# Three-pass fp32 projections on one NeuronCore: high and low activations as one 512-column operand, sums of the two halves added outside TensorE

## The chip, the core and the metric

The kernel runs on one core of a Trainium2 chip. The metric is the device time of one launch in microseconds (us); lower is better. The core's engines work on their own instruction streams and meet at semaphores: PE (TensorE, matmuls into PSUM), DVE (VectorE), ACT (ScalarE), POOL (GpSimd) and SP, which starts most DMAs. PSUM has 8 banks of 128 partitions x 512 fp32.

## The reference, cut to what matters

Two transformer blocks over 256 tokens of width 1024, all in fp32. The part that the change touches are the projections whose results are needed with features on the partitions: keys and queries of all attentions, and the input of the pooling mixer.

```python
def memory_attention(xq, mem_k, mem_v): ...     # softmax(q k^T / sqrt(128)) v, 4 heads
def pool_layer(h, w_in, w_group, scale, w_out, mem_k, mem_v):
    proj = h @ w_in
    u, xq = proj[..., :D_MODEL], proj[..., D_MODEL:]
    mix = multiscale_pool(u, w_group, scale)
    return jnp.concatenate([mix, memory_attention(xq, mem_k, mem_v)], axis=-1) @ w_out
def diff_layer(...):    # q, k, v, xq = h @ w_in ; two softmaxes a head, their difference times v
def second_block(...):
    proj = rms_norm(x, g_pre_mix) @ w_in         # q, k, v of MoBA and of retention
    mq, mk = rotary(mq), rotary(mk)              # rq, rk too
    ...
    c = cross_attention(h, mem_n, w_cq, w_ckv, w_co)
```

Between these mixers stand five gated feed-forward layers (1024 x 5632 and 2816 x 1024 each), which the change leaves alone.

## The kernel before, in words

**Arithmetic.** Each fp32 product is made of three matmuls of a rounded type (fp32r): a number is split into a high part and a low part (the rest), and high x high, high x low and low x high are summed in PSUM. ACT makes the high part of a chunk of weights (`w_hi`, L1468), DVE the low part (`w_lo`, L1702).

**Chunks.** All weights come as 238 blocks of 128 x 2048 numbers through a ring of three slots. `Plan` lists them with all other work; every engine walks the same list of items, so the order on each engine is that of the list. A "cols" chunk (`project`) is a projection with features first: 8 contraction tiles (kt) x 2 halves of 128 output features x 3 passes = 48 matmuls, each with 128 x 128 weights standing and 256 tokens moving (`column_passes`, L1119 to L1121). There are 34 such chunks: 10 around the pooling layer (2 keys, 2 queries xq, 4 of u, 2 more keys), 10 in the differential attention (4 q, 4 k, 2 xq), 6 at MoBA and retention (q0, k0, q2, k2, k4, k6 below), 4 keys of the second memory, and 4 queries of the cross-attention. Other chunks have the activations standing and 512 columns of weights moving (`token_passes`, L1125 to L1129, 24 matmuls a chunk).

**Banks.** Two PSUM banks, prod0 and prod1, hold products. A cols chunk fills one of them with both halves (256 + 256 columns); the next takes the other. DVE reads a finished bank in one instruction (L1874, L1876, or two at L1880) that multiplies by `rb`, the token's 1/rms, and signals `prod_read`. So a bank has a whole chunk's time to be read. `rb` is made by PE and ACT at a "spread" item (L1441, L1645) from a statistic that POOL finishes (L1062).

**Order around a cols chunk.** ACT and DVE first split the weights of a later chunk ("flush"), then take the chunk's result. In the attention layers a chunk is "opened": PE does part 0 (kt 0 to 3), then a "tick" of attention work (scores S, weighted values V, transposes T), then part 1. DVE's share of a tick is maxima (L1825, L1821), softmax weights (L1787 to L1802) and low parts of outputs (L1813). Rotation of q and k (L1989 to L1992) and the pooling windows (L2006 to L2017) are DVE work that stands between the chunks. The first chunk that takes new activations is "fresh": PE waits for each low part `acts_l` (L1728).

## Time and profile before

| what | value |
|---|---|
| median of 3 runs | 1423.87 us (1423.79 to 1424.02) |
| span of the profiled execution | 1422.5 us |
| PE busy | 1405.2 us, 99% |
| DVE busy | 856.5 us, 60% |
| ACT busy | 704.0 us, 49% |
| mean granted TensorE clock | 1.000 |

The span runs from the first to the last instruction; the timed runs are 1.4 us longer, which is what lies around it. Busy time of PE counts overlapping matmuls once; a matmul's own duration is longer than its step to the next one, so paces are read from starts. "Idle before" names what an engine waited for.

### The profile page before, as it was taken

The page shows a single profiled execution, that of the slowest core. Times are in us where ns is not written, and L with a number is a line of the kernel's source. Part 1 is how long each engine was busy: PE and PEld are TensorE (multiplying, and loading weights), DVE is VectorE, ACT ScalarE, POOL GpSimd, SP SyncE. Part 2 cuts the span into 40 slices and gives each one's busy share as a digit, 9 for nine tenths or more (in the row PEclk, how much of TensorE's full clock was granted, in tenths as well). Part 3 has the DMA queues.
Part 4 walks back from the last instruction along what each step waited for, and adds up shares of the span by engine and source line. Part 5 has one row for each costly group of instructions (what it writes and reads, how often), then busy time and mean ns, then how long its engine had stood idle before and what let it go on. Part 6 is the DMA issues. An engine that isn't in the chain of part 4 may idle for free.

```text
span 1422.5 us, 18638 instructions
## 1 busy us (share of the span) xinstructions
PE 1405.2 (99%) x7200; PEld 1189.8 (84%) x7200; DVE 856.5 (60%) x1029; ACT 704.0 (49%) x975; POOL 255.9 (18%) x504
## 2 busy tenths in 40 slices
PE   8999999999999999999999999999999999999998
PEld 6888889988888888888889888888887989788886
DVE  5655565756555565555656565555796655565554
ACT  6545455355444454444555555444655554544442
POOL 1022210002222222222012113222200100132222
PEclk9999999999999999999999999999999999999999
DMA  9756554455665656665544347665544554356562
GB/s 355 276 195 218 198 186 174 152 204 174 220 215 197 210 202 209 210 218 200 179 149 150 120 173 267 207 224 206 183 168 146 191 179 136 138 196 231 198 220 74
DMA packets 71223, 275.55 MB, mean 194 GB/s; under 512 B 17344, under 2 KB 37184, under 8 KB 40288
## 3 DMA queue, kind: packets, MB, share of 16 engines
q1 hardware_dynamic: 56736, 259.57, 51.8%
q0 software_dynamic: 14400, 14.81, 3.4%
q8 instruction: 57, 0.93, 0.3%
q14 instruction: 30, 0.25, 0.1%
HBM read 259.88 MB, written 1.05 MB: 183 GB/s over the span
## 4 chain that ended last, share of the span: by engine, by line
PE 93%; ACT 2%; DVE 2%; DMA 1%; issue 1%; SPq 0%; POOL 0%; DVEq 0%; POOLq 0%; ACTq 0%
PE prod L1125 15%; PE prod L1129 15%; PE prod L1126 15%; PE acc L1129 10%; PE acc L1125 10%; PE acc L1126 10%; PE prod L1119 4%; PE prod L1120 4%; PE prod L1121 4%; PE acc L1323 1%; DMA raw<-in_weights_dram 1%; ACT w_hi L1468 1%; PE acc L1144 1%; PE acc L1343 1%; DVE w_lo L1702 1%
## 5 line engine op out<-in xcount | busy, mean ns | idle before, releaser
L1702 DVE TENSOR_TENSOR w_lo<-raw,w_hi 128x2048 fp32r<-128x2048 f32 x235 | 538.1, 2291 | 402.2 <-ACT w_hi L1468 399.8
L1468 ACT CAST w_hi<-raw 128x2048 fp32r<-128x2048 f32 x235 | 447.9, 1907 | 434.1 <-PE prod L1129 179.7
L1125 PE MATMUL prod<-w_hi,acts_h 128*128 128x512 f32 x944 | 370.6, 393 | 3.1 <-DVE four L1858 1.1
L1129 PE MATMUL prod<-w_hi,acts_l 128*128 128x512 f32 x944 | 367.7, 390 | 0.0
L1126 PE MATMUL prod<-w_lo,acts_h 128*128 128x512 f32 x944 | 367.4, 389 | 0.0
L995 POOL DMA_DIRECT2D four<-four x408 | 200.1, 498 | 608.6 <-DVE four L1862 591.5
L1125 PE MATMUL acc<-w_hi,mix_h 128*128 128x512 f32 x600 | 236.1, 394 | 0.0
L1129 PE MATMUL acc<-w_hi,mix_l 128*128 128x512 f32 x600 | 233.7, 390 | 0.0
L1126 PE MATMUL acc<-w_lo,mix_h 128*128 128x512 f32 x600 | 233.5, 389 | 0.0
L1125 PEld LDWEIGHTS prod<-w_hi,acts_h 128*128 128x128 f32 x944 | 177.2, 188 | 44.8 <-issue 6.2
L1129 PEld LDWEIGHTS prod<-w_hi,acts_l 128*128 128x128 f32 x944 | 177.2, 188 | 37.5 <-DVE acts_l L1772 0.3
L1126 PEld LDWEIGHTS prod<-w_lo,acts_h 128*128 128x128 f32 x944 | 177.3, 188 | 35.8
L1129 PEld LDWEIGHTS acc<-w_hi,mix_l 128*128 128x128 f32 x600 | 112.6, 188 | 23.6
L1125 PEld LDWEIGHTS acc<-w_hi,mix_h 128*128 128x128 f32 x600 | 112.7, 188 | 23.0 <-issue 0.2
L1126 PEld LDWEIGHTS acc<-w_lo,mix_h 128*128 128x128 f32 x600 | 112.7, 188 | 22.8
L1119 PE MATMUL prod<-acts_h,w_hi 128*128 128x256 f32 x424 | 124.0, 293 | 1.1 <-ACT work L1532 0.7
L1121 PE MATMUL prod<-acts_h,w_lo 128*128 128x256 f32 x424 | 119.9, 283 | 0.0
L1120 PE MATMUL prod<-acts_l,w_hi 128*128 128x256 f32 x424 | 119.8, 283 | 0.0
L1547 ACT ACTIVATE four<-prod,stats 128x256 f32<-128x256 f32 x108 | 51.1, 474 | 116.6 <-PE prod L1129 107.4
L1119 PEld LDWEIGHTS prod<-acts_h,w_hi 128*128 128x128 f32 x424 | 81.1, 191 | 3.6 <-issue 2.4
L1120 PEld LDWEIGHTS prod<-acts_l,w_hi 128*128 128x128 f32 x424 | 81.2, 191 | 0.4 <-issue 0.2
L1121 PEld LDWEIGHTS prod<-acts_h,w_lo 128*128 128x128 f32 x424 | 81.0, 191 | 0.0
(275 smaller groups left out, 1181.7 us busy)
## 6 DMA issues: line engine op xcount, KB each, us to landing
raw<-in_weights_dram SPq DMA_DIRECT2D x235, 1024.0 KB, 5.0
four<-four SPq DMA_DIRECT2D x408, 16.0 KB, 2.1
four<-four POOLq DMA_DIRECT2D x408, 16.0 KB, 1.9
raw<-in_weights_dram SPq DMA_DIRECT2D x12, 256.0 KB, 6.7
work<-in_mem_dram POOLq DMA_DIRECT2D x2, 1024.0 KB, 13.0
grow<-in_gain_rows_dram POOLq DMA_DIRECT2D x4, 512.0 KB, 3.6
tabs<-in_tabs_dram POOLq DMA_DIRECT2D x1, 1632.0 KB, 10.0
work<-in_x_t_dram SPq DMA_DIRECT2D x4, 256.0 KB, 5.5
```

The source lines that it names most:

```text
L995: engine.dma_start(mid_moved_to[32 * b:32 * b + 32, a * P:(a + 1) * P], mid_blocks[32 * a:32 * a + 32, b * P:(b + 1) * P]).then_inc(done, 16)
L1119: pe.matmul(out, wh, moving_hi, start=first, stop=False, skip_group_check=True)
L1120: pe.matmul(out, wh, moving_lo, start=False, stop=False, skip_group_check=True)
L1121: return pe.matmul(out, wl, moving_hi, start=False, stop=last, skip_group_check=True)
L1125: pe.matmul(out, still_hi, wh, start=first, stop=False, skip_group_check=True)
L1126: pe.matmul(out, still_hi, wl, start=False, stop=False, skip_group_check=True)
L1129: return pe.matmul(out, still_lo, wh, start=False, stop=last, skip_group_check=True)
L1144: mm = pe.transpose(bank[:, i * S + t * P:i * S + (t + 1) * P], x[:, t, kt * P:(kt + 1) * P], ident)
L1323: mm = pe.matmul(bank[:, at:at + width], dests[q][r0:r1, qt + n, t * P:(t + 1) * P], dests[k][r0:r1, kt + n, 0:width], start=(n == 0), sto ...
L1468: act.copy(w_hi[:, c % RING], raw[:, c % RAW]).then_inc(hi_done, 1)
L1547: act.activation(gate_s[:, t], up_bank(it, t)[:, 0:S], ACT.Silu, scale=rstd["x"][:, t:t + 1]).then_inc(silu_done, 1)
L1702: dve.tensor_tensor(w_lo[:, c % RING], raw[:, c % RAW], w_hi[:, c % RING].bitcast(F32), ALU.subtract).then_inc(lo_done, 1)
```

## The change

A cols chunk now works half by half. Half 0 (128 features) goes to prod0 and half 1 to prod1. For each kt one matmul of the high weights takes the high and the low activations side by side, 2 x 256 = 512 columns (both parts now lie in one tensor, `acts` or `mix`, 8 KB or 12 KB apart), and leaves two sums in the bank: columns 0 to 255 for the high, 256 to 511 for the low activations. Then 8 matmuls of the low weights add to the first sum. So 32 matmuls a chunk stand for 48. ACT copies the second sum to the destination (`correction`), DVE adds the first to it and multiplies by `rb` in a second instruction (`feature_half`). A bank is given back, by `halves_read`, after the add. The old whole-bank read is gone. In a fresh chunk the high matmuls of both halves come first (kt 0-1, 2-3, 4-7) and all low weights last. PE now starts a cols chunk when `w_hi` is there and waits for `w_lo` only ahead of the low weights.

```diff
     def project(self, source, col, dest, at, of="x", mid=None, factors=None):
-        self.chunk("cols", (*source, "cols", col), mid, dest=dest, at=at, of=of, e=self.e, factors=factors,
-                   acts=self.acts if of == "x" else self.mem, free=self.bank_free(1))
+        self.chunk("cols", (*source, "cols", col), mid, dest=dest, at=at, of=of, n=self.read, factors=factors,
+                   acts=self.acts if of == "x" else self.mem, free=self.bank_free(2))
         self.used(of)
-        self.to_read(1)
+        self.read += 1
+        for half in range(2):
+            self.bank_reader.append(("halves_read", 2 * self.read - 1 + half))
+        self.e += 2
...
+                def high_passes(half, kts):
+                    if kts[0] == 0:
+                        reader(pe, it["free"][half])
+                    for kt in kts:
+                        if fresh and half == 0:
+                            pe.wait_ge(lo_done_of, it["acts"] if it["of"] == "mem2" else it["acts"] - KT + kt + 1)
+                        at = kt * COLS + half * P
+                        pe.matmul(prod[half], w_hi[:, slot, at:at + P], both[:, :, base + kt], start=kt == 0,
+                                       stop=False, skip_group_check=True)
+                def low_passes(half):
+                    if half == 0:
+                        pe.wait_ge(lo_done, c + 1)
+                    for kt in range(KT):
+                        at = kt * COLS + half * P
+                        mm = pe.matmul(prod[half][:, 0], w_lo[:, slot, at:at + P], hi[:, base + kt], start=False,
+                                       stop=kt == KT - 1, skip_group_check=True)
+                    mm.then_inc(chunk_used if half else features_done, 1)
+                if fresh:
+                    for kts in (range(0, 2), range(2, 4), range(4, 8)):
+                        for half in range(2):
+                            high_passes(half, kts)
+                        turn_pending()
+                    for half in range(2):
+                        low_passes(half)
+                else:
+                    for half in parts:
+                        high_passes(half, range(KT))
+                        low_passes(half)
+                        turn_pending()
...
+            def correction(it, half):
+                if half:
+                    act.wait_ge(chunk_used, it["c"] + 1)
+                else:
+                    act.wait_ge(features_done, it["n"] + 1)
+                act.copy(feature_out(it, half), prod[half][:, 1]).then_inc(correction_out, 1)
...
+            def feature_half(it, half):
+                out, n = feature_out(it, half), 2 * it["n"] + half + 1
+                dve.wait_ge(correction_out, n)
+                dve.tensor_tensor(out, prod[half][:, 0], out, ALU.add).then_inc(halves_read, 1)
+                dve.wait_ge(halves_read, n)
+                if half == 0:
+                    dve.wait_ge(rb_done, it["rb"])
...
+                    ins = dve.tensor_tensor(out, out, r, ALU.mult)
+                if half:
+                    ins.then_inc(prod_read, 1)
```

On ACT and DVE `correction(0)` and `feature_half(0)` stand behind the flush of the "open" item, or, where a chunk isn't opened, behind the flush of the chunk itself with half 1 right after.

DVE at the entrance of MoBA, before (q0 and k0 are the first two cols chunks on the new x, `work` holds q and k; in brackets what an instruction waits for):

```order
L1928 TENSOR_TENSOR x_res<-x_res,grow 128x512 x3
L1702 TENSOR_TENSOR w_lo<-raw,w_hi 128x2048 [waits hi_done,rstd_done]
L1874 TENSOR_TENSOR work<-prod0,rb 128x512 [waits chunk_used,rb_done]
L1702 TENSOR_TENSOR w_lo<-raw,w_hi 128x2048 [waits hi_done]
L1874 TENSOR_TENSOR work<-prod1,rb 128x512 [waits chunk_used,rb_done]
L1952 SCALAR_TENSOR_TENSOR mix_l<-obuf,vecs,mix_h 128x256 [waits mem_hi] x4
```

The same place on DVE after the change:

```order
L1977 TENSOR_TENSOR x_res<-x_res,grow 128x512 x3
L1746 TENSOR_TENSOR w_lo<-raw,w_hi 128x2048 [waits hi_done,rstd_done]
L1825 TENSOR_TENSOR work<-prod0,work 128x256 [waits correction_out]
L1834 TENSOR_TENSOR work<-work,rb 128x256 [waits rb_done,halves_read]
L1825 TENSOR_TENSOR work<-prod1,work 128x256 [waits correction_out]
L1834 TENSOR_TENSOR work<-work,rb 128x256 [waits halves_read]
L1746 TENSOR_TENSOR w_lo<-raw,w_hi 128x2048 [waits hi_done]
L1825 TENSOR_TENSOR work<-prod0,work 128x256 [waits correction_out]
L2001 SCALAR_TENSOR_TENSOR mix<-obuf,vecs,mix 128x256 [waits mem_hi] x4
```

The add that gives back prod0 stands behind the `w_lo` that waits for `rstd_done`, and the add that gives back prod1 behind the multiply that waits for `rb_done` (k0's other three instructions repeat q0's and are left out).

PE at the same place after the change, from q0's last high matmuls to k0's end (before, k0 was 48 matmuls into prod1 with only `mid_done` and `lo_done` to wait for, and the two matmuls of the spread, L1441, in their middle):

```order
L1196 MATMUL prod1<-acts,w_hi 128x512 x4
L1204 MATMUL prod0<-acts,w_lo 128x256 [waits lo_done]
L1204 MATMUL prod0<-acts,w_lo 128x256 x7
L1204 MATMUL prod1<-acts,w_lo 128x256 x8
L1196 MATMUL prod0<-acts,w_hi 128x512 [waits halves_read,hi_done]
L1196 MATMUL prod0<-acts,w_hi 128x512 x7
L1471 MATMUL aux<-tabs,stats 128x128 [waits rb_done,rstd_done]
L1196 MATMUL prod1<-acts,w_hi 128x512 [waits halves_read]
L1196 MATMUL prod1<-acts,w_hi 128x512 x7
L1204 MATMUL prod1<-acts,w_lo 128x256 x8
```

k0's half 0 now waits for q0's prod0, its half 1 for q0's prod1, and the spread, from which `rb` comes, stands between them.

DVE at the end of the pooling projections, before (behind the read of u's last chunk; L2006 to L2017 are one window of the pooling):

```order
L1702 TENSOR_TENSOR w_lo<-raw,w_hi 128x2048 [waits hi_done]
L1874 TENSOR_TENSOR mem_k<-prod0,rb 128x512 [waits chunk_used,rb_done]
L2006 TENSOR_TENSOR work<-work 128x2x256 [waits prod_read,pooled]
L2006 TENSOR_TENSOR work<-work 128x2x256 [waits dve_step]
L2011 SCALAR_TENSOR_TENSOR work<-work 128x512 [waits dve_step]
```

The same place after:

```order
L1746 TENSOR_TENSOR w_lo<-raw,w_hi 128x2048 [waits hi_done]
L1825 TENSOR_TENSOR mem_k<-prod0,mem_k 128x256 [waits correction_out]
L1834 TENSOR_TENSOR mem_k<-mem_k,rb 128x256 [waits rb_done,halves_read]
L1825 TENSOR_TENSOR mem_k<-prod1,mem_k 128x256 [waits correction_out]
L1834 TENSOR_TENSOR mem_k<-mem_k,rb 128x256 [waits halves_read]
L2055 TENSOR_TENSOR work<-work 128x2x256 [waits prod_read,pooled]
```

One instruction has become four, and PE's next chunk needs the first of them.

## Rows read from the trace of the kernel before

**Rows 1.** Page, parts 1 and 2: busy us; tenths of the granted clock.

```profile
PE 1405.2 (99%) x7200; PEld 1189.8 (84%) x7200; DVE 856.5 (60%) x1029; ACT 704.0 (49%) x975; POOL 255.9 (18%) x504
PEclk9999999999999999999999999999999999999999
```

**Rows 2.** Groups by form, PE: the two groups of cols high passes.

```profile
L1119 PE MATMUL prod<-acts_h,w_hi 128*128 128x256 f32 x424 | 124.0, 293 | 1.1 <-ACT work L1532 0.7 <-DVE acts_l L1728 0.4
L1119 PE MATMUL prod<-mix_h,w_hi 128*128 128x256 f32 x128 | 36.3, 284 | 0.0
```

**Rows 3.** Timeline, PE, in an xq chunk: start, duration, engine, line.

```profile
219.15 0.28 PE L1119 MATMUL prod<-acts_h,w_hi 128*128 128x256 f32 x1
...
222.75 0.28 PE L1119 MATMUL prod<-acts_h,w_hi 128*128 128x256 f32 x1
```

**Rows 4.** Timeline, PE, in a chunk with 512 columns moving.

```profile
178.30 0.39 PE L1125 MATMUL acc<-w_hi,mix_h 128*128 128x512 f32 x1
...
187.14 0.39 PE L1125 MATMUL acc<-w_hi,mix_h 128*128 128x512 f32 x1
```

**Rows 5.** Groups, DVE: whole-bank read, and 256 columns of PSUM with SBUF.

```profile
L1874 DVE TENSOR_TENSOR work<-prod,rb 128x512 f32<-128x512 f32 x14 | 9.6, 688 | 14.5 <-PE prod L1121 14.5
L1813 DVE TENSOR_TENSOR mix_l<-o_bank,mix_h 128x256 fp32r<-128x256 f32 x14 | 5.5, 416 | 0.0
```

**Rows 6.** Line L1645, ACT: copy of 256 columns, ns min/median/max.

```profile
L1645 ACT COPY rb<-aux x6: 363/373/374, 100.9 to 1171.2; 128x256 f32<-128x256 f32 x6
```

**Rows 7.** Timeline, DVE, MoBA's entrance.

```profile
1018.83 2.49 DVE L1928 TENSOR_TENSOR x_res<-x_res,grow 128x512 f32<-128x512 f32 x4
1023.53 2.29 DVE L1702 TENSOR_TENSOR w_lo<-raw,w_hi 128x2048 fp32r<-128x2048 f32 x1 [2.21 <-POOL stats L1062]
1025.74 0.68 DVE L1874 TENSOR_TENSOR work<-prod,rb 128x512 f32<-128x512 f32 x1
...
1038.60 2.28 DVE L1702 TENSOR_TENSOR w_lo<-raw,w_hi 128x2048 fp32r<-128x2048 f32 x1
```

**Rows 8.** Timeline, PE, the same place: k0's start, the spread, the first scores.

```profile
1020.77 0.28 PE L1119 MATMUL prod<-acts_h,w_hi 128*128 128x256 f32 x1
...
1023.64 0.62 PE L1441 MATMUL aux<-tabs,stats 128*128 128x128 f32 x4
1024.02 0.36 PE L1119 MATMUL prod<-acts_h,w_hi 128*128 128x256 f32 x1
...
1039.07 0.93 PE L1323 MATMUL acc<-work 64*128 64x128 f32 x8 [1.03 <-DVE work L1992]
```

**Rows 9.** Windows (us, then busy us of PE, PEld, DVE, ACT, POOL; clock): three stretches.

```profile
254.00:276.00 22.00, 22.00 (x169) 21.25 (x168) 21.29 (x36) 9.42 (x11) 0.00 (x0) 1.00 0.36 122
1023.00:1039.00 16.00, 15.04 (x83) 12.80 (x81) 15.27 (x20) 8.31 (x11) 1.10 (x2) 1.00 0.58 204
1039.00:1078.00 39.00, 38.74 (x294) 33.92 (x294) 35.40 (x84) 21.21 (x47) 0.00 (x0) 1.00 0.49 170
```

**Rows 10.** Timeline, DVE, end of the pooling projections: u read, splits behind it.

```profile
253.62 0.69 DVE L1874 TENSOR_TENSOR work<-prod,rb 128x512 f32<-128x512 f32 x1 [3.94 <-PE prod L1121]
...
258.74 2.29 DVE L1702 TENSOR_TENSOR w_lo<-raw,w_hi 128x2048 fp32r<-128x2048 f32 x1
...
270.76 2.28 DVE L1702 TENSOR_TENSOR w_lo<-raw,w_hi 128x2048 fp32r<-128x2048 f32 x1
```

**Rows 11.** Timeline, PE, the same place: tick before u's last chunk, first chunk behind.

```profile
253.35 0.60 PE L1379 MATMUL o_bank<-four,mem_v 128*128 128x256 f32 x2
...
272.79 0.40 PE L1125 MATMUL prod<-w_hi,mix_h 128*128 128x512 f32 x1
```

**Rows 12.** Timeline, differential attention: split behind k0, PE's wait at q1.

```profile
700.34 1.91 ACT L1468 CAST w_hi<-raw 128x2048 fp32r<-128x2048 f32 x1 [3.63 <-PE prod L1121]
...
714.32 0.35 PE L1119 MATMUL prod<-acts_h,w_hi 128*128 128x256 f32 x1 [0.72 <-ACT work L1532]
```

**Rows 13.** Timeline, DVE, the read of the first chunk of keys.

```profile
201.67 0.68 DVE L1874 TENSOR_TENSOR mem_k<-prod,rb 128x512 f32<-128x512 f32 x1
```

More of the change, by code:

```diff
@@ L281, in bank_free @@
         return [self.bank_reader[e - 2] if e >= 2 else None for e in range(self.e, self.e + n)]
-    def to_read(self, n):
-        for _ in range(n):
-            self.read += 1
-            self.bank_reader.append(("prod_read", self.read))
-        self.e += n
     def ffn_down(self, source, p):
@@ L960, in group_bank, with feature_out @@
             return (prod[it["e"] % 2], prod[(it["e"] + 1) % 2], aux[:].rearrange("p (a b) -> p a b", a=2), o_bank)[g]
+        def feature_out(it, half):
+            if it["dest"] == "u":
+                return padded[:, it["at"] + half, PAD:PAD + S]
+            return dests[it["dest"]][:, it["at"] + half]
         def reader(engine, told):
@@ L1132, in operand @@
                 if of == "x":
-                    return acts_lo, acts_h, acts_l, 0
-                return mem_lo, mix_h, mix_l, mem_base[of]
+                    return acts_lo, acts_h, acts_l, acts, 0
+                return mem_lo, mix_h, mix_l, mix, mem_base[of]
             def turn_half(it, h):
@@ L1176, in columns_chunk @@
             def columns_chunk(it, parts):
-                lo_done_of, hi, lo, base = operand(it["of"])
-                slot, bank = it["c"] % RING, prod[it["e"] % 2]
-                if 0 in parts:
-                    reader(pe, it["free"][0])
-                for kt in [kt for part in parts for kt in range(4 * part, 4 * part + 4)]:
-                    if seen[it["of"]] < it["acts"]:
-                        pe.wait_ge(lo_done_of, it["acts"] if it["of"] == "mem2" else it["acts"] - KT + kt + 1)
-                    for half in range(2):
-                        mm = column_passes(bank[:, half], slot, kt * COLS + half * P, hi[:, base + kt],
-                                           lo[:, base + kt], kt == 0 and half == 0, kt == KT - 1)
-                    if kt == 1:
+                lo_done_of, hi, _, both, base = operand(it["of"])
@@ new lines, in columns_chunk @@
+                slot, c = it["c"] % RING, it["c"]
+                fresh = seen[it["of"]] < it["acts"]
+                def high_passes(half, kts):
[7 more added lines that the diff above has]
+                                       stop=False, skip_group_check=True)
@@ L1277, in chunk @@
                     if it["c"] >= RAW:
-                        pe.wait_ge(lo_done, it["c"] + 1)
+                        pe.wait_ge(hi_done if it["kind"] == "cols" else lo_done, it["c"] + 1)
                     for told in it["late_readers"]:
@@ L1508, in _ @@
                     flush()
+                    if kind == "open" and it["chunk"]["kind"] == "cols":
+                        correction(it["chunk"], 0)
                 elif kind in ("up", "cols", "rows_half", "down", "group"):
@@ L1550, in _ @@
                             flush()
+                    elif kind == "cols":
+                        if not it["opened"]:
+                            correction(it, 0)
+                        correction(it, 1)
                     elif kind == "group":
@@ L1837, in _ @@
                     flush()
+                    if it["chunk"]["kind"] == "cols":
+                        feature_half(it["chunk"], 0)
                 elif kind in ("up", "cols", "rows_half", "down", "group"):
```

46 lines of the change are left out of this document (20 added, 26 removed).

## Prediction

> **What bounds the kernel now.** I read the page first, then groups, then the timeline where DVE is densest. PE is busy 1405.2 us of 1422.5 [rows 1], so the kernel is a queue of matmuls with hardly a gap: a matmul saved shortens the time if nothing new makes PE wait, and each new wait of PE is added in full. DVE is at 60% over the span [rows 1], but not evenly: 21.29 of 22 us at the end of the pooling projections, 15.27 of 16 at MoBA's entrance, 35.40 of 39 in the run behind it [rows 9]. There DVE has no room, and there the change gives it work and lets PE wait for it. The account is therefore: one pace, and then the places where a bank comes back late.
>
> **The pace of a cols chunk.** Matmuls with 256 columns start 3.60 us apart over 30 of them: 0.120 us each [rows 3]. With 512 columns it is 8.84 us over 39: 0.227 us each [rows 4]. So a step is about 0.013 us plus the columns, and joining two saves one 0.013. A chunk takes 48 x 0.120 = 5.76 us now and 16 x 0.227 + 16 x 0.120 = 5.55 us after: 0.21 us less. The groups of high passes hold 424 + 128 = 552 matmuls [rows 2], 34 chunks x 16 and 8 of the pooling's group chunk, which stays. 34 x 0.21 = **7.2 us** less. No row has 512 columns in two pieces 8 KB apart. Bounds: 0.227 as in [rows 4], or two separate steps, 0.240, as in [rows 3], which would take 16 x 34 x 0.013 = 7.2 us back. I take 0.227, since that row is a moving operand of the same size and type.
>
> **What a chunk costs ACT and DVE.** ACT: two copies of 0.37 [rows 6]. DVE: instead of one read of 0.69 [rows 5], two adds of 0.42 (PSUM with SBUF, 256 columns [rows 5]) and two multiplies of the same size. Each multiply waits for its add, so little overlaps: 0.8 us a half, 1.6 a chunk, 1.0 us more than now. A bank comes free after: 0.27 from the end of PE's half to the reader (PE's next matmul at 253.35 [rows 11], the read at 253.62 [rows 10]), copy 0.37, add 0.42, in all 1.1 us, if both engines stand ready. PE wants that bank when the other half, 2.8 us, is done. Normally that is covered. It isn't in a fresh chunk, where half 0 ends only 8 x 0.12 = 0.96 us before half 1, nor where the engine is held up ahead of the add.
>
> **MoBA's entrance (2 chunks, q0 and k0).** Now: k0 starts at 1020.77 in the other bank, while DVE waits for POOL's statistic till 1023.53, splits weights for 2.2 us and reads q0 at 1025.74 [rows 7, 8]; nobody minds. After: (a) q0's last `acts_l` is there when DVE goes on to L1928, 1018.9 [rows 7], as before; behind it PE still has 1 + 4 high and 16 low matmuls, 1.1 + 1.9 = 3.0 us, so q0 ends at 1022.0. (b) k0's half 0 needs prod0, whose add stands behind that same wait and split: 1025.75 + 0.42 = 1026.2. PE stands for 4.2 us. (c) Half 0 runs to 1029.0, the spread to 1029.4 (its place in PE's order, 0.38 long, 1023.64 to 1024.02 [rows 8]). Only then does ACT copy `rb` (1030.1), and DVE multiply, add q0's half 1 and free prod1 at 1031.0. PE stands for another 1.6 us. (d) DVE's chain to the rotated keys, which runs now without a gap from 1023.53 to the end of the rotation at 1038.60 [rows 7, 9] and for which the first scores wait at 1039.07 [rows 8], becomes 3.9 us of waiting for `rb`, 2.0 us of extra instructions and small waits longer, less what overlaps: it ends at 1044.4, the scores start at 1044.9. PE is there at about the same time, so nothing more is lost. Net **+5.8 us**, the pace of both chunks and today's 1.03 us of idle PE included.
>
> **The run behind it (4 chunks).** DVE has 3.6 us free in 39 [rows 9], gets 4 us more, and its order puts the add and multiply of half 0 ahead of the softmax weights and the rotation. Walking the queues with the durations now: the transposes behind k2 wait for weights (about 1.7 us), the scores behind k4 for the rotation (1.7 us). From this go the pace of four chunks, 0.8, and gaps of today and work that hides a part. Net **+1.4 us** at the rows_half chunk behind k6.
>
> **The end of the pooling projections (3 chunks).** Call T the end of u's last but one chunk (253.35 now). From there DVE works without a gap: 253.62 to the end of the split at 270.76 + 2.2 = 272.96 [rows 10], 19.3 us, of which three reads 1.8; the new instructions up to the add that frees the bank for the chunk behind are 4.5 us, and the first starts 0.64 after PE: T + 0.64 + 19.3 - 0.2 idle - 1.8 + 4.5 = T + 22.5. PE gets there now at 272.79, T + 19.4 [rows 11], and could at T + 18.8. It is held three times, each time by prod0 behind a split: about 1.4, 1.9 and 0.5 us. Net **+3.1 us**.
>
> **The differential attention (10 chunks).** q0 is fresh like MoBA's q0: 1.2 us of low passes behind the last `acts_l`. Behind k0 the row is: PE's last matmul, ACT's split at 700.34, DVE's split, maxima, exponentials, PE at 714.32 after 0.72 us of idle [rows 12]; the copy of half 1 (0.37) now stands ahead of that split, so q1 starts 1.1 us later than now in sum. Further on ACT's squares for the head norms stand behind a copy that waits for half 0; then POOL, DVE's scaling and PE's turn come later by 1.2 us. Pace gives back most of the rest. Net **+1.5 us**.
>
> **The other 15 chunks.** Keys of the first memory (2): the read at 201.67 stands behind a split [rows 13], k1 needs the bank at 201.3 and gets it at 202.1: +0.9 net. The last 13: -0.21 each, -2.8, and against it three fresh chunks whose successor waits 0.3 us and one turn of x that comes 0.35 late: -1.9 net.
>
> Sum: 5.8 + 1.4 + 3.1 + 1.5 + 0.9 - 1.9 = **+10.8 us**. The span goes from 1422.5 to 1433.3; with the 1.4 us around it, and equally from the median 1423.9, **1434.7 us**. Weights are no new bound: a chunk of 5.55 us asks no more of the DMAs than today's 512-column chunks (24 x 0.227 = 5.44 us).
>
> **Rivals.**
> (A) *The banks are never missed* (not slower). Mechanism: the add gets done within the other half's 2.8 us everywhere, because DVE's waits and splits turn out movable. Then only the pace is left: 1423.9 - 7.2 = **1416.7 us**. It decides at k0 of MoBA: if PE starts k0's half 0 before 1023.5 it holds. Against it: the order shows the add behind `rstd_done`. A sentence of the Trainium skill speaks for it: TensorE: Matmul & The Clock Gate, HAM oscillation, tells of a kernel in which PSUM double buffering "gave no further gain", which would make its loss free. Here DVE's full stretches [rows 9] contradict that. 6%.
> (B) *Only the entrances bite.* In the dense runs DVE's added work falls into gaps I took as filled. Then MoBA's run, the pooling's end and the differential attention keep their pace (-0.8, -0.6, and +1.2 + 0.4 - 2.1 = -0.5 instead of +1.4, +3.1, +1.5): 1434.7 - 7.9 = **1426.8 us**. For: the replay adds small waits in one direction. Against: 21.29 of 22. 13%.
> (C) *The clock falls in the new pause.* Every row has the granted clock at 1.00 [rows 1, 9] and PE's longest wait in the rows is 1.03 us [rows 8]; one of 4.2 us has no row. At the lower of the two levels k0's half 0 takes 2.8 us more and all of DVE's chain behind it moves: **1437.5 us**, or 1440.3 if half 1 runs so too. The Trainium skill (the same page, Why this matters for your kernels) says that gaps of idle PE between bursts bring the clock down to 1.2 GHz; the trace of before doesn't show it. 15%.
> (D) *The joined operand isn't read at the pace of one.* Two pieces cost two steps: **1441.9 us**. 5%.
>
> **How the numbers follow.** The forecast has 61%, with its own spread of about 3 us either way (eight places, each read to some tenths): 1431.5 to 1438. Range: 1426 to 1440.5; it leaves out A, D, the end of C and the outer half of B's spread. About 0.2% (2.8 us) is what a measurement of this kernel tells from no change. Faster by that, below 1421.0: A, 6%. Within, to 1426.7: half of B and a tail of the forecast, 9%. Slower: 85%.
>
> **What would show each step.** Pace: the high matmuls 0.227 us apart and 0.120 for the low ones; the former at 0.24 means D. Entrance: PE idle some 4 us ahead of q0's successor, released by DVE's add, then some 1.6 us; the first MoBA scores 5.8 us later relative to q0's start. Pooling's end: three waits of PE for the add, together near 4 us. PE not busy: 1422.5 - 1405.2 = 17.3 us now, after it 17.3 + 10.8 + 7.2 = 35 us. Granted clock under 1.00 behind the pause means C. I am wrong if PE's new waits sum to less than 7 us, or if they stand at places other than adds that free a bank, weights and rotations.

## The result

| | before | changed |
|---|---|---|
| median | 1423.94 us (1423.79 to 1424.34, 4 runs) | 1442.51 us (1441.90 to 1442.92, 4 runs) |
| span of the profiled execution | 1422.5 us | 1441.1 us |
| PE busy | 1405.2 us | 1407.6 us |
| PE not busy | 17.3 us | 33.5 us |
| DVE busy | 856.5 us | 886.9 us |

The ratio is 1.0129, 95% interval 1.0118 to 1.0141: 18.6 us slower. The forecast was 10.8 us slower, 1434.7 us, and its range ended at 1440.5 us. The sign and the places were right, the size was not: 7.8 us are missing from it.

The page of the changed kernel, parts 1 and 2, against [rows 1]:

```profile
PE 1407.6 (98%) x6656; PEld 1163.2 (81%) x6656; DVE 886.9 (62%) x1127; ACT 725.7 (50%) x1043; POOL 257.1 (18%) x504
PEclk9999999999999999999999999999999999999999
```

544 matmuls are gone and PE is busy 2.4 us longer; the other 16.2 us are time in which PE isn't busy. The row of the clock shows nothing: a slice is 36 us, and the fall lasted 6.8 us.

PE's waits, with what ended them: us in all, times, longest. These are the first nine rows.

```profile
PE prod L1196 <- DVE work L1825: 6.1, 3, 4.0
PE prod L1196 <- DVE mem_k L1825: 2.5, 2, 1.8
PE acc L1373 <- DVE sq L1850: 1.8, 1, 1.8
PE acc L1163 <- DVE x_res L1809: 1.7, 1, 1.7
PE acc L1353 <- DVE work L2041: 1.4, 1, 1.4
PE prod L1196 <- DVE acts L1772: 1.4, 2, 0.7
PE aux L1373 <- DVE mix L2094: 1.3, 1, 1.3
PE acc L1151 <- DVE x_res L1794: 1.3, 3, 0.5
PE aux L1437 <- POOL mem_v L1042: 1.3, 1, 1.3
```

L1825 is the add that gives a bank back: 8.6 us in its two rows. L1850 are softmax weights, L2041 the rotation: the added work made them late. Not all rows are new: the list of the kernel before has, under its own line numbers, the waits for L1809 (1.7 us), L2094 (1.3) and L1042 (1.3) too. Read this view for the places, not for the sum: small delays don't stand in it, and neither does time at a lower clock.

**MoBA's entrance**, PE (the answer to [rows 8]): q0's high matmuls, k0's half 0, the spread, k0's half 1, the first scores.

```profile
1025.03 2.60 PE L1196 MATMUL prod<-acts,w_hi 128*128 128x512 f32 x8 [0.69 <-DVE acts L1772]
...
1033.55 3.75 PE L1196 MATMUL prod<-acts,w_hi 128*128 128x512 f32 x8 [4.01 <-DVE work L1825]
...
1038.81 0.75 PE L1471 MATMUL aux<-tabs,stats 128*128 128x128 f32 x4
...
1040.88 2.11 PE L1196 MATMUL prod<-acts,w_hi 128*128 128x512 f32 x8 [1.32 <-DVE work L1825]
...
1055.09 0.93 PE L1353 MATMUL acc<-work 64*128 64x128 f32 x8
```

The same eight matmuls take 3.75 us behind the pause of 4.01 us and 2.11 us behind that of 1.32. The windows of this stretch (us, then busy us of PE, PEld, DVE, ACT, POOL; then the granted clock) say why:

```profile
1024.00:1028.00 4.00, 3.31 (x15) 2.14 (x14) 3.98 (x9) 2.40 (x8) 1.89 (x4) 1.00 0.60 203
1028.00:1034.00 6.00, 1.99 (x14) 1.82 (x14) 3.18 (x3) 3.74 (x9) 1.69 (x4) 0.86 0.37 127
1034.00:1037.00 3.00, 3.00 (x8) 2.33 (x8) 0.00 (x0) 0.00 (x0) 0.00 (x0) 0.50 0.94 317
1037.00:1040.00 3.00, 2.56 (x13) 2.27 (x12) 0.00 (x0) 0.74 (x2) 0.00 (x0) 0.65 0.08 33
1040.00:1044.00 4.00, 3.09 (x17) 2.58 (x17) 3.87 (x6) 0.02 (x1) 0.00 (x0) 1.00 0.00 0
```

0.50 is 1.2 of 2.4 GHz. From 1034 to 1037 DVE, ACT and POOL do nothing: they wait for PE, which runs at half its clock. DVE there (the answer to [rows 7]):

```profile
1030.77 2.29 DVE L1746 TENSOR_TENSOR w_lo<-raw,w_hi 128x2048 fp32r<-128x2048 f32 x1 [2.22 <-POOL stats L1069]
1032.98 0.42 DVE L1825 TENSOR_TENSOR work<-prod,work 128x256 f32<-128x256 f32 x1
1040.07 0.42 DVE L1834 TENSOR_TENSOR work<-work,rb 128x256 f32<-128x256 f32 x1 [6.67 <-ACT rb L1689]
1040.41 0.42 DVE L1825 TENSOR_TENSOR work<-prod,work 128x256 f32<-128x256 f32 x1
```

The add of half 0 stands behind the statistic and a split, the add of half 1 behind `rb`, which comes from PE's own spread.

**Where the time went.** Starts of the same instruction of PE in both traces, subtracted; each row is what the shift grew by in that stretch.

| stretch | last pair of starts | measured | forecast |
|---|---|---|---|
| up to the first memory's keys | - | -0.1 | 0 |
| keys of the first memory | 206.73, 207.79 | +1.2 | +0.9 |
| end of the pooling projections | 272.79, 276.43 | +3.0 | +3.1 |
| differential attention | 793.20, 800.46 | +3.6 | +1.5 |
| MoBA's entrance | 1039.07, 1055.09 | +8.8 | +5.8 |
| run behind it | 1070.17, 1088.77 | +2.6 | +1.4 |
| the last 13 chunks | 1203.20, 1221.68 | -0.5 | -1.9 |
| sum | | +18.5 | +10.8 |

The rows are rounded; unrounded they sum to 18.48. The 13 chunks lie in two places: -0.4 at the first xq and u, -0.1 at the second memory and the cross-attention.

**The pace.** Timeline, PE, keys of the second memory in the changed kernel, one row for eight matmuls:

```profile
1148.09 2.08 PE L1196 MATMUL prod<-mix,w_hi 128*128 128x512 f32 x8
1150.01 1.12 PE L1204 MATMUL prod<-mix,w_lo 128*128 128x256 f32 x8
1150.96 2.00 PE L1196 MATMUL prod<-mix,w_hi 128*128 128x512 f32 x8
1152.80 1.12 PE L1204 MATMUL prod<-mix,w_lo 128*128 128x256 f32 x8
```

From start to start a steady half is 1.84 + 0.96 = 2.80 us, 0.230 us a high and 0.120 us a low matmul. A steady chunk takes 5.59 us against 5.76: 0.17 us gained, not 0.21. The fresh chunk ahead of these rows began at 1142.34 and took 5.75 us: nothing gained. Its half 0 is done only 8 low matmuls before PE wants that bank again for the next chunk, so PE is held there.

### The profile page after: what moved, and what is told of

It reads as the page before. It is cut to its first block, busy times and chain, and to the rows that moved or that the text cites. A ratio compares the mean times of both kernels' runs of the same rounds, so it can differ in the third digit from the quotient of the medians.

```text
span 1441.1 us, 17716 instructions
## 1 busy us (share of the span) xinstructions
PE 1407.6 (98%) x6656; PEld 1163.2 (81%) x6656; DVE 886.9 (62%) x1127; ACT 725.7 (50%) x1043; POOL 257.1 (18%) x504
## 3 DMA queue, kind: packets, MB, share of 16 engines
HBM read 259.88 MB, written 1.05 MB: 181 GB/s over the span
## 4 chain that ended last, share of the span: by engine, by line
PE 87%; DVE 6%; ACT 3%; issue 2%; DMA 1%; SPq 0%; POOL 0%; DVEq 0%; POOLq 0%; ACTq 0%
PE prod L1132 15%; PE prod L1136 15%; PE prod L1133 15%; PE acc L1136 9%; PE acc L1132 9%; PE acc L1133 9%; PE prod L1196 6%; PE prod L1204 3%; DVE w_lo L1746 2%; DMA raw<-in_weights_dram 1%; ACT w_hi L1498 1%; PE acc L1353 1%; ACT four L1703 1%; DVE acts L1772 1%; PE acc L1151 1%
## 5 line engine op out<-in xcount | busy, mean ns | idle before, releaser
L1132 PE MATMUL prod<-w_hi,acts 128*128 128x512 f32 x944 | 370.6, 393 | 3.2 <-DVE w_lo L1754 1.2
L1136 PE MATMUL prod<-w_hi,acts 128*128 128x512 f32 x944 | 367.7, 390 | 0.0
L1133 PE MATMUL prod<-w_lo,acts 128*128 128x512 f32 x944 | 367.5, 389 | 0.0
L1132 PE MATMUL acc<-w_hi,mix 128*128 128x512 f32 x600 | 236.1, 393 | 0.0
L1136 PE MATMUL acc<-w_hi,mix 128*128 128x512 f32 x600 | 233.8, 390 | 0.0
L1133 PE MATMUL acc<-w_lo,mix 128*128 128x512 f32 x600 | 233.5, 389 | 0.0
L1132 PEld LDWEIGHTS prod<-w_hi,acts 128*128 128x128 f32 x944 | 177.2, 188 | 44.7 <-issue 7.6
L1136 PEld LDWEIGHTS prod<-w_hi,acts 128*128 128x128 f32 x944 | 177.2, 188 | 37.6 <-DVE acts L1816 0.3
L1133 PEld LDWEIGHTS prod<-w_lo,acts 128*128 128x128 f32 x944 | 177.3, 188 | 35.7
L1136 PEld LDWEIGHTS acc<-w_hi,mix 128*128 128x128 f32 x600 | 112.6, 188 | 23.7
L1132 PEld LDWEIGHTS acc<-w_hi,mix 128*128 128x128 f32 x600 | 112.7, 188 | 22.8
L1133 PEld LDWEIGHTS acc<-w_lo,mix 128*128 128x128 f32 x600 | 112.7, 188 | 22.7
L1196 PE MATMUL prod<-acts,w_hi 128*128 128x512 f32 x416 | 111.9, 410 | 7.8 <-DVE work L1825 5.3
L1196 PEld LDWEIGHTS prod<-acts,w_hi 128*128 128x128 f32 x416 | 75.6, 191 | 27.1 <-issue 7.5
```

What stands on the lines that cost most here:

```text
L1132: pe.matmul(out, still_hi, wh, start=first, stop=False, skip_group_check=True)
L1133: pe.matmul(out, still_hi, wl, start=False, stop=False, skip_group_check=True)
L1136: return pe.matmul(out, still_lo, wh, start=False, stop=last, skip_group_check=True)
L1196: pe.matmul(prod[half], w_hi[:, slot, at:at + P], both[:, :, base + kt], start=kt == 0, stop=False, skip_group_check=True)
```

## Experiments

Lines in the profiles of most variants are up to some tens higher than in the changed kernel; the operations are the same. "Old form" is that of the kernel before. "Shift" is, as in the table, how much later an instruction of PE starts than in the kernel before. Medians are to be held against 1442.51 (changed) and 1423.9 to 1424.3 (before, run each time beside them).

### The entrance

**e1.** q0 and k0 in the old form.

```diff
     def project(self, source, col, dest, at, of="x", mid=None, factors=None):
+        old = self.projects in OLD
...
+        if old:
+            self.bank_reader.append(("prod_read", self.read))
+            self.e += 1
+            return
...
+OLD = [20, 21]
```

> Changed kernel with q0 and k0 at MoBA's entrance in the old form (48 matmuls, one bank, one read by DVE), the other 32 cols chunks in the new form. Theory 1 (the entrance loses through the bank behind DVE's wait and through the clock): the first MoBA scores come 8.8 us earlier than in the changed kernel (their shift against the kernel before is then +7.2, not +16.0), the granted clock stays at 1.00, the time is 1442.5 - 8.8 = 1433.7 us. Rival (DVE's stretch behind the entrance is full in either form, so that PE only waits a little later): less than 6 us come back, 1436.5 us or more, and PE's waits in the four chunks of the run grow by the rest.

Measured: 1433.32 us (1432.9 to 1433.6), 9.2 us less, and the granted clock stays at 1.00 there, both as expected (1433.7). In the trace the shift is 6.9 us when q0 begins and 6.8 us at the first scores. The whole loss of the entrance is local to two chunks of 34.

**e2.** PE's pause filled with matmuls that nobody reads.

```diff
                 elif kind == "open":
+                    if it["fill"]:
+                        reader(pe, it["fill"])
+                        pe.wait_ge(hi_done, it["chunk"]["c"] + 1)
+                        for n in range(30):
+                            pe.matmul(aux[:, 0:S], w_hi[:, it["chunk"]["c"] % RING, 0:P], acts_h[:, n % KT], start=True, stop=True)
                     chunk(it["chunk"], (0,))
```

> Changed kernel with 30 more matmuls of 256 columns into the unused auxiliary bank (30 x 0.12 = 3.6 us of work whose result nobody reads) where PE stood still for 4.0 us ahead of k0's half 0. Theory 1 (the pause is what lowered the clock): granted clock 1.00 there, k0's half 0 takes 2.8 instead of about 5.2 us, the time is 2.5 us less than that of the changed kernel, 1440.0 us. Rival (the fall has another cause, for instance DVE's and ACT's load there, or costs nothing because the chain on DVE decides anyway): 1442.5 us.

Measured: 1440.32 us (1440.15 to 1442.28; three of the four runs lie within 0.2 us, the fourth has no trace). PE's timeline and the window behind:

```profile
1029.32 3.76 PE L1447 MATMUL aux<-acts,w_hi 128*128 128x256 f32 x30
1033.49 2.08 PE L1196 MATMUL prod<-acts,w_hi 128*128 128x512 f32 x8 [0.41 <-DVE work L1830]
...
1038.29 2.11 PE L1196 MATMUL prod<-acts,w_hi 128*128 128x512 f32 x8 [1.33 <-DVE work L1830]
```

```profile
1034.00:1037.00 3.00, 2.97 (x19) 2.49 (x17) 0.00 (x0) 0.37 (x1) 0.00 (x0) 1.00 0.97 328
```

k0's half 0 starts when it did before (1033.49 for 1033.55), runs at full clock, and half 1 starts 2.59 us earlier. The bank came back at the same moment, so nothing but the clock was taken away: it costs 2.6 us at this place (2.2 us between the medians), and a busy PE prevents it. This was rival (C) of the prediction. The Trainium skill (TensorE: Matmul & The Clock Gate, Why this matters for your kernels) says that gaps of idle PE bring the clock down to 1.2 GHz; by that, the traces agree here. The falls behind shorter pauses, in e5 and e8 below, are known from these traces alone.

**e5 and e6.** DVE's wait for the statistic left out; then also one multiply for both halves, behind both adds.

```diff
                         dve.tensor_tensor(x[:, t, cols], x[:, t, cols], grow[:, cols], ALU.mult).then_inc(xf_done, 1)
-                    dve.wait_ge(rstd_done, it["n"] + 1)
...
                 dve.tensor_tensor(out, prod[(it["e"] + half) % 2][:, 0], out, ALU.add).then_inc(halves_read, 1)
+                if not half:
+                    return
                 dve.wait_ge(halves_read, n)
...
+                dve.wait_ge(rb_done, it["rb"])
...
-                if half == 0:
-                    dve.wait_ge(rb_done, it["rb"])
...
+                    ins = dve.tensor_tensor(out, out, bcast(r, 2), ALU.mult)
```

> Changed kernel, DVE doesn't wait for POOL's statistic behind the four multiplies of x at MoBA's entrance (the multiply by rb, which needs that statistic, waits for rb anyway). Its next split of weights can then start at 1028.6 instead of 1030.8 in the changed kernel's own time, and the add behind it 2.2 us earlier. Theory 1 (that wait, passed on by the add, makes PE's pause, and the pause lowers the clock): PE's 4.0 us ahead of k0's half 0 become 1.8, the granted clock stays at 1.00 there, 2.2 + 2.5 us less: 1437.9 us. Rival (ACT's squares and its copies behind them hold the add just as long): the pause stays over 3 us, the clock falls, 1441 us or more.

> As e5_no_stat_wait, and in all 34 chunks DVE adds half 0, later half 1, and multiplies both halves by rb in one instruction of 512 columns behind the second add, so that no add stands behind rb, and 34 instructions go. Theory 1: PE's second wait at the entrance (1.3 us, for the add behind the multiply that needs rb) goes too, and DVE saves about 0.85 - 0.7 = 0.15 us a chunk where it has no room: 1.0 to 1.5 us less than e5_no_stat_wait, 1436.6 us. Rival (the chain to the rotated keys on DVE sets the time there, and the later multiply takes back what the earlier add gives): the same as e5_no_stat_wait.

Measured: e5 1438.47 us (1437.97 to 1440.06), e6 1435.10 us (1434.66 to 1435.50). PE at k0's half 0 and half 1 in e5, and at k0's half 0 in e6:

```profile
1031.60 2.06 PE L1222 MATMUL prod<-acts,w_hi 128*128 128x512 f32 x8 [1.71 <-DVE work L1876]
...
1036.38 2.11 PE L1222 MATMUL prod<-acts,w_hi 128*128 128x512 f32 x8 [1.32 <-DVE work L1876]
```

```profile
1030.07 2.06 PE L1222 MATMUL prod<-acts,w_hi 128*128 128x512 f32 x8 [1.71 <-DVE work L1876]
```

One wait of DVE less takes 2.3 us from the pause, and behind the 1.71 us that are left the clock stays at 1.00: both as expected for e5. But the profiled execution, the longest of the four (1440.06 us; the others 1437.97 to 1438.72), has a fall of the clock elsewhere, in the run, behind a pause of the size that the changed kernel has there too (1.77 us) without a fall. The eight matmuls behind it and the window:

```profile
1067.27 0.63 PE L1399 MATMUL acc<-tabs,sq 128*128 128x128 f32 x3 [1.75 <-DVE sq L1901]
1067.57 3.67 PE L1222 MATMUL prod<-acts,w_hi 128*128 128x512 f32 x8
```

```profile
1068.00:1070.00 2.00, 2.00 (x6) 1.52 (x6) 1.97 (x3) 0.70 (x2) 0.00 (x0) 0.50 0.04 8
```

That costs 1.6 us in this execution, so a pause of some 1.7 us is one that the clock sometimes survives and sometimes doesn't. The kernel before has one too, 1.68 us at 1231.5, with the clock at 1.00.

e6 gained 3.4 us on e5 and not 1.0 to 1.5. Held trace against trace, k0's half 1 starts 1.6 us earlier, of which a new wait behind it takes 1.0 back; the differential attention gives 1.3 us, the run 1.0 us beside the 1.6 of the clock. That was the first sign that the dense stretches had been sized too small. I took it for 0.15 us a chunk less on DVE, come through nearly whole; but the edit also moves 0.43 us of DVE's work from ahead of a tick to behind it, and e14 below speaks for that as the reason.

**e11.** The same wait left out of the kernel before.

> Kernel before, old form in all 34 chunks, with DVE's wait for the statistic behind the four multiplies of x left out, as in e5. Theory 6 (in the kernel before DVE's row from 1023.53 to the rotated keys has no gap, so 2.2 us less of waiting ahead of it moves the first scores until PE's own work bounds them; PE's idle time there is 1.03 us): 1.0 us less, 1423.0 us. Rival (rb, not the wait, starts that row): no change, 1424.0 us.

Measured: 1424.25 against 1424.15 us, ratio 1.0001 (0.9992 to 1.0010). The 1.0 us didn't come; the rival holds. DVE's timeline:

```profile
1020.94 2.28 DVE L1702 TENSOR_TENSOR w_lo<-raw,w_hi 128x2048 fp32r<-128x2048 f32 x1
1025.53 0.69 DVE L1874 TENSOR_TENSOR work<-prod,rb 128x512 f32<-128x512 f32 x1 [2.31 <-ACT rb L1645]
```

The split runs 2.6 us earlier than in [rows 7], and then DVE waits 2.31 us for `rb`. The read of q0 starts at 1025.53 for 1025.74. In the kernel before that wait hid behind another one; it cost time only when a bank's release was put behind it.

### The dense stretches

**e9.** The ten chunks of the differential attention and the four of the run in the old form (as e1, with other numbers in the list).

> Changed kernel with the ten chunks of the differential attention and the four of MoBA's and retention's run (q2, k2, k4, k6) in the old form; the 20 others, MoBA's entrance among them, in the new one. Theory 5 (each place costs by itself what the shift between the two traces shows there): the shift grows by 3.6 us in the differential attention and by 2.6 us in the run, so 6.2 us come back: 1442.5 - 6.2 = 1436.3 us. Rival (in the dense places the loss is the lateness of the entrance and goes with it, or a place that is mended sends its wait on to the next one): less than 4 us come back, 1438.5 us or more.

Measured: 1435.64 us (1435.33 to 1435.90), 6.9 us less (6.2 expected). Against the changed kernel's trace the shift grows by 3.6 us over the differential attention and 2.6 us over the run, the figures of the table. The pause at the entrance is 4.01 us as before and the clock falls as before: the places are independent and add up.

**e14.** The multiply of half 0 left out in those 14 chunks.

```diff
                 if half == 0:
                     dve.wait_ge(rb_done, it["rb"])
+                    if 10 <= it["site"] < 20 or 22 <= it["site"] < 26:
+                        return
```

> Changed kernel without the multiply by rb of half 0 (0.43 us of DVE) in the ten chunks of the differential attention and the four of MoBA's and retention's run; half of the keys and queries is unscaled there, nothing else changes. Theory 5a (in the dense places the loss is DVE's added instruction time, which passes to PE nearly whole: e6 took 0.15 us a chunk from DVE there and the shift grew by 1.3 us less over ten chunks): 14 x 0.43 = 6.0 us less of DVE's time, of which 60 to 90% come back: 1437.1 to 1438.9 us. Rival 5b (the loss there is the place of the add and the copy in the order, and of the splits, not their length): at most 1.5 us come back, 1441 us or more.

Measured: 1439.66 us (1439.20 to 1440.30), 2.9 us less: 47% of the 6.0 us, between the two theories. By place: 1.6 of the 3.6 us in the differential attention, 1.05 of the 2.6 us in the run. PE's waits there, changed kernel, then e14 (end of the differential attention, then softmax weights in the run):

```profile
791.14 0.65 PE L1487 MATMUL aux<-tabs,sq 128*128 128x128 f32 x4 [1.09 <-DVE sq L2079]
...
1071.73 0.55 PE L1373 MATMUL acc<-tabs,sq 128*128 128x128 f32 x3 [1.77 <-DVE sq L1850]
1079.59 0.93 PE L1353 MATMUL acc<-work 64*128 64x128 f32 x8 [1.39 <-DVE work L2041]
```

```profile
1069.14 0.55 PE L1399 MATMUL acc<-tabs,sq 128*128 128x128 f32 x3 [1.18 <-DVE sq L1903]
```

The wait for the weights falls by 0.59 us. So the multiply of half 0, 0.43 of the 1.0 us that the change adds to DVE in a chunk, is a little under half of the loss. Is it its length or its place? e6 keeps a multiply of both halves in these chunks, but behind the tick, and saves 1.3 us in the differential attention and 1.1 us in the run, against 1.6 and 1.05 us with the multiply left out. So most of what it costs is its place ahead of the tick's softmax weights. 1.2 us are the fresh pair q0 and k0 of the differential attention, which e14 leaves unmoved. How the rest divides between the order of copies and adds and the time still added stays open.

### The order of adds and splits

**e7 and e8.** Copy and add of half 0 ahead of the split of weights, in all chunks; e8 with the repairs of e6 as well.

```diff
                 if kind == "open":
-                    flush()
                     if it["chunk"]["kind"] == "cols":
                         feature_half(it["chunk"], 0)
+                    flush()
...
+                    if kind == "cols" and not it["opened"] and not it["old"]:
+                        feature_half(it, 0)
                     if not early:
```

> Changed kernel with its stat wait, but ACT copies and DVE adds and multiplies half 0 of every cols chunk ahead of the split of weights that stood before them. It reaches the chunks without a tick in the middle that have a split there: keys, xq, the end of the pooling projections, the entrances. Theory 4 (at the end of the pooling projections and at the keys of the first memory PE waits since the add stands behind a 2.2 us split): the waits for mem_k's add (2.5 and 0.4 us) go, 2 us of it as time; at MoBA's entrance the add comes 2.2 us earlier, the pause is 1.8 us and the clock stays: 1442.5 - 2.0 - 4.7 = 1435.8 us. Rival (the weights, split later, come late instead): the waits for w_lo grow by as much, 1440 us or more.

> Changed kernel with the three repairs of order together: no wait for the statistic ahead of the adds, one multiply behind both adds, adds ahead of the split. Theory 1 and 4: the entrance costs 1.6 us instead of 8.8, the end of the pooling projections and the keys 2 us less: 1442.5 - 7.2 - 2.5 = 1432.8 us, still slower than the kernel before (1423.9), since DVE has more to do and PE's other waits stay. Rival (order was all that was wrong, the banks are never missed once the adds stand first): 1423 us or less.

Measured: e7 1466.49 us (1464.05 to 1468.26), e8 1453.82 us (1453.51 to 1455.91). The times expected for them were too low by 31 and 21 us. DVE in e7, in u's chunks with a tick:

```profile
244.25 0.42 DVE L1876 TENSOR_TENSOR work<-prod,work 128x256 f32<-128x256 f32 x1 [1.35 <-ACT work L1548]
244.71 0.43 DVE L1885 TENSOR_TENSOR work<-work,rb 128x256 f32<-128x256 f32 x1
245.05 2.28 DVE L1774 TENSOR_TENSOR w_lo<-raw,w_hi 128x2048 fp32r<-128x2048 f32 x1
247.25 0.16 DVE L1899 RECIPROCAL small<-small 128x2 f32<-128x2 f32 x1
247.44 0.62 DVE L1901 TENSOR_SCALAR four<-four,small 128x256 f32<-128x256 f32 x2
```

I had overlooked that a split stands in opened chunks too. DVE now waits for half 0 first, and the split then runs between the add and the softmax weights, for which PE waits. The split needs nothing from the running chunk, so ahead of the add it fills that wait. By place, e7's shift grows by 3.2 us at u, 8.7 in the differential attention, 11.4 at the entrance and 14.3 in the run. But at the end of the pooling projections, where the step was aimed, it grows by nothing, for 3.0 us in the changed kernel. The longer pauses also bring the clock down: its mean over the span is 0.992 in e7 and 0.995 in e8, against 0.997 in the changed kernel. By the mean clocks that is at most some 7 of the 24 us in e7, an estimate (0.005 x 1466).

**e10 and e13.** The same step only in chunks without a tick, on top of e6; e13 leaves out the second memory and the cross-attention.

> As e6_one_multiply, and copy and add of half 0 ahead of the split of weights only in the chunks that have no tick in the middle (keys, first xq, the two chunks at the end of the pooling projections, q0 and k0 of the differential attention, q0 of MoBA, keys of the second memory, first query of the cross-attention). In e7 the same step in chunks with a tick put a split between the add and the softmax weights. Theory 4, narrowed: the waits for mem_k's add (2.3 us and 0.7 us) go and nothing comes for them: 1435.1 - 3.0 = 1432.1 us. Rival (late splits take it back here too): 1435 us or more.

> As e10_repairs_closed, but the keys of the second memory and the first query of the cross-attention keep the order of e6 (split, then copy and add). In e10 the start of that stretch came 2.55 us earlier than in e6, and behind it PE waited anew for an add (0.82 us), for x (1.45) and for the scores' operand (1.61). Theory 4, narrowed again: those three waits come from the moved split alone: 1435.1 - 2.5 = 1432.6 us. Rival (the stretch gives the gain back whatever stands in it, since DVE's work there is what bounds PE): 1435 us.

Measured: e10 1437.38 us (1437.11 to 1438.32), e13 1432.86 us (1432.44 to 1433.01). e10 is 2.55 us ahead of e6 when the second memory begins, and then PE waits anew:

```profile
1141.79 2.11 PE L1222 MATMUL prod<-mix,w_hi 128*128 128x512 f32 x8 [0.82 <-DVE mem_k L1876]
1160.22 1.09 PE L1161 MATMUL acc<-tabs,x_res 128*128 128x128 f32 x8 [1.45 <-DVE x_res L1815]
...
1192.58 1.99 PE L1379 MATMUL acc<-mem_k,work 128*128 128x256 f32 x8 [1.61 <-DVE work L1889]
```

That is the rival of e10, which had put it at 1435 us or more. With that stretch left alone e13 comes out 0.3 us from its expectation. By place, e13 against e6: the keys of the first memory cost 0.5 us instead of 1.2, the end of the pooling projections 0.8 instead of 2.9, the entrance 2.3 instead of 3.3. So the split ahead of the add was a cause in these places, and the main one in the first two. The first xq and the fresh pair of the differential attention, where the split moved too, lose 1.1 and 0.5 us more than in e6. The order of waits, adds and splits, the one multiply and the clock that no longer falls together make 9.7 us of the 18.6 (1442.51 to 1432.86); with the new form in all chunks e13 is still 8.5 us slower than the kernel before.

### The pace

**e3.** High and low activations next to one another.

```diff
-        acts = sb("acts", [P, 2, KT, S], F32R)
-        acts_h, acts_l = acts[:, 0], acts[:, 1]
+        acts = sb("acts", [P, KT, 2, S], F32R)
+        acts_h, acts_l = acts[:, :, 0], acts[:, :, 1]
```

> Changed kernel with the high and low activations of a contraction tile next to one another (acts laid out 8 x 2 x 256), so that the 512 moving columns of 28 of the 34 chunks are one contiguous piece instead of two pieces 8 KB apart; the 6 chunks on the memories keep the two pieces. Theory 2 (the two pieces are why a step is 0.233 us and not 0.227): 28 x 16 x 0.006 = 2.7 us less, 1439.8 us, and a half's high matmuls 0.227 us apart. Rival (the step is what a matmul with 128 x 128 standing weights and 512 columns takes, wherever they lie): 1442.5 us and the same steps.

Measured: 1442.32 us (1441.86 to 1442.85), no change. Timeline, PE, second half of the second xq chunk:

```profile
227.90 2.00 PE L1196 MATMUL prod<-acts,w_hi 128*128 128x512 f32 x8
229.74 1.12 PE L1204 MATMUL prod<-acts,w_lo 128*128 128x256 f32 x8
```

Again 1.84 us for eight. A moving operand in two pieces 8 KB apart costs nothing against one piece.

**e4 and e12.** The new form only where nothing waits: twelve chunks; then nine, without the fresh ones, with one multiply and without the statistic's wait.

> New form in only the 12 chunks where no wait of PE was seen to grow: xq (2), u3 and u2, the four keys of the second memory and the four queries of the cross-attention; the other 22 in the old form. Theory 3 (the gain is 0.12 us a chunk where nothing waits): 12 x 0.12 = 1.4 us less than before, 1422.5 us, less 0.3 us for each of up to three fresh chunks: 1422.5 to 1423.4. The forecast's pace of 0.21 us a chunk: 2.5 us less, 1421.4. Rival (ACT's and DVE's extra work costs PE the gain even here): 1423.9 us or more.

> Best mixture by what was measured: new form in nine chunks that are neither fresh nor in a place where PE came to wait (second xq, u3, u2, the last three keys of the second memory, the last three queries of the cross-attention), one multiply for both halves, the old form in the other 25, and no wait for the statistic. Theory 3 (a steady chunk gains 0.13 to 0.17 us, a fresh one nothing): 9 x 0.15 = 1.3 us less, 0.4 of it lost again at the turn of x behind the keys of the second memory, and 1.0 us from the wait: 1422.2 us. Rival (the form gains nothing anywhere, the wait alone does): as e11_before_no_stat_wait.

Measured: e4 1423.57 against 1424.17 us, ratio 0.9996 (0.9987 to 1.0005); e12 1423.33 against 1424.15 us, 0.9995 (0.9986 to 1.0003). The medians are 0.6 and 0.8 us lower, but neither interval excludes no change. e4 lies 0.2 us above its expectation, e12 1.1 us above: 1.0 us of it was for the statistic's wait, which e11 shows to be worth nothing. In e4's trace the keys of the second memory gain 0.44 us, and the turn of x behind them (PE's transposes of the new x, for which it waits for DVE) takes 0.53 back:

```profile
1148.80 1.09 PE L1161 MATMUL acc<-tabs,x_res 128*128 128x128 f32 x8
1150.13 1.09 PE L1161 MATMUL acc<-tabs,x_res 128*128 128x128 f32 x8 [0.23 <-DVE x_res L1815]
```

No version was found that beats the kernel before by more than can be measured.

## Why the prediction was right and wrong

The range was missed through these terms of the sum: the clock behind the new pause, put at nothing in it (3.0 us with the rest of the entrance), the differential attention and the run, sized too small (2.1 and 1.2 us), and the pace with the chunks that were to gain by it (1.4 us in the last 13). With +0.3 us at the keys of the first memory, and -0.1 each at the start and at the end of the pooling projections, that is the missing 7.8 us.

- **What bounds the kernel**: right. PE is still the queue, and its waits make 16.2 of the 18.6 us. PE's idle time was forecast at 35 us and is 33.5, but that nearness is no proof of the sum: by the forecast PE would be busy 1405.2 - 7.2 = 1398.0 us, and it is 1407.6. What was missed stands in PE's busy time: the slower clock, the gain that didn't come and the small delays.
- **The pace**: forecast gain too large. The step of 0.227 us held to 0.003 (1.84 us for eight, turn to the low weights included), but the gain of 0.21 us is itself a small difference, so these thousandths make it 0.17. And I counted it for 34 chunks, though six are fresh and gain nothing. 28 x 0.17 = 4.8 us, not 7.2, worked out from the steady rows (and 34 chunks at the forecast's own steps make 7.1). (D) is refuted by e3 and by the rows.
- **MoBA's entrance**: waits right, sum wrong. 4.2 and 1.6 us of pauses were forecast, 4.01 and 1.32 measured. What the sum left out was what the first pause does to the clock. I had it as a rival with 15% and charged 2.8 us; it is 2.6 us (e2). 5.8 + 2.6 = 8.4 of 8.8. The mistake was to give a consequence of my own term a small chance: having forecast a pause four times as long as any in the rows (the trace has one of 1.68 us, which I hadn't shown), I should have asked first what the clock does in it, and had no row that said it stays.
- **The run and the differential attention**: mis-sized. +1.4 and +1.5 forecast, +2.6 and +3.6 measured and confirmed by e9. The named waits came (the softmax weights 1.77 for 1.7 us, the rotation 1.39 for 1.7), but "pace gives back most of the rest" failed: the pace was smaller, and delays of 0.1 to 0.2 us, which no list of waits shows, ate it. In the differential attention the fresh pair cost 1.2 us and q1's start 0.3; from there to the last tick the pace gave back nothing (+0.25); the turn behind the head norms came 1.2 us later, as forecast, and then 0.7 us more, which I hadn't forecast. That the extra DVE work ahead of a tick's weights is part of it, e14 and e6 show; the small delays by themselves were not tested.
- **The end of the pooling projections**: right in place, order and cause (e13), and 3.0 for 3.1 us in sum. That the sum is so near is partly luck: the three waits were 0.77, 1.75 and 0.35 us, 2.9 for a forecast of 3.8, and the pace, which was to give 0.6 back, didn't. Here the replay went instruction by instruction from one row to the next, in a stretch where DVE has no gap.
- **The keys of the first memory**: +1.2 for +0.9; PE waited 0.74 us for the add, as named.
- **The last 13 chunks**: -0.5 for -1.9. The gain at the second memory was taken back at the turn of x, which waits for DVE.
- **Rivals**: (C) happened, on top of the forecast; by itself it would have given 1437.5 us, so it doesn't explain the miss alone. (A) is refuted with the order as it is and with it repaired (e13). (B) is refuted by e9.

## What to carry to other kernels

When a forecast contains a new pause of the matmul engine longer than any in the trace, price its clock in the forecast, not as a rival: here 4 us of idleness cost 2.6 us more, and 1.75 us cost 1.6 in one execution, while pauses of that length cost nothing in others. When a bank is handed over twice as often, look at what stands ahead of the instruction that returns it: a statistic's wait, a multiply and a split that cost nothing while a bank had a whole chunk of time were behind most of 9.7 us here. A gain of 0.17 us in a chunk of 5.76 is easily spent on one added instruction of 0.4 us, so count the time of the helping engine where it is full before counting matmuls.

## What the hardware showed

- The granted clock was 0.50 behind the pause of 4.01 us, also for k0's first 512-column matmuls, and the same in e3, e9 and e14 with the same pause. Pauses of 1.68 to 1.77 us left it at 1.00 (the kernel before at 1231.5; e5 and e6 at the entrance; the changed kernel in the run and, 1.75 us, at the end of the pooling projections), and so did one of 2.00 us in e7. But it fell behind one of 1.75 us in e5, and in e8 behind 1.44 and 0.23 us at the turn of x, where e10 had 1.45 us without a fall. So the length of a pause of this size doesn't decide; that was new to me.
- Eight matmuls with 512 moving columns, with the turn to 256 columns behind them, take 1.84 us from start to start, with their columns in one piece or in two pieces 8 KB apart.
- 544 matmuls fewer made PE's busy time 2.4 us longer. Even without the 2.6 us at half the clock it fell by only 0.2 us: the ends are modelled, and small delays lie inside what counts as busy.
